# Applying the mean and the inverse deviation of two layer norms on the activation engine, one row tile later on the vector engine

## The reference, cut to what matters

```python
def _standardize(x):
    mu = mean(x); var = mean(square(x - mu))
    return (x - mu) * rsqrt(var + LN_EPS)

def _layer_norm(x, gain, bias):
    return _standardize(x) * gain + bias

# second block
x = _layer_norm(ALPHA * x + (1.0 + g1) * mix, ln1_gain, ln1_bias)
h = _standardize(x) * (1.0 + sc2) + sh2          # a second norm, of the result of the first
f = _conv_glu_ffn(h, w_ffn_up, w_ffn_conv, b_ffn_conv, w_ffn_down)
x = _layer_norm(ALPHA * x + (1.0 + g2) * f, ln2_gain, ln2_bias)   # this is the output
```

## Time and profile before

| what | value |
|---|---|
| median of 3 runs | 1673.8 us (1672.94 to 1674.36) |
| the profiled execution: time | 1674.36 us |
| its span, first to last instruction | 1672.4 us |
| PE busy | 1525.9 us, 91% of the span |
| DVE busy | 879.7 us, 53% |
| ACT busy | 582.6 us, 35% |
| POOL busy | 643.0 us, 38% |

### The profile page before, as it was taken

How to read it: one execution, slowest core, us unless ns; L and a number is a source line. 1 busy time by engine, 2 the same in 40 slices (tenths; PEclk the granted TensorE clock), 3 DMA queues, 4 the chain that set the end, 5 groups by cost and what they waited for, 6 DMA issues and landing times. The chain is left out here.

```text
span 1672.4 us, 19643 instructions
## 1 busy us (share of the span) xinstructions
PE 1525.9 (91%) x7216; PEld 1226.2 (73%) x7216; DVE 879.7 (53%) x1484; ACT 582.6 (35%) x856; POOL 643.0 (38%) x456
## 2 busy tenths in 40 slices
PE   4999989787999999997998999988994999999996
PEld 3776855676888788875877777777883888888885
DVE  4672378625858777397462255424548332333337
ACT  4332377115222121215341463444426332232231
POOL 2432200032655545562542224224551434544442
PEclk9999989898999999997997998998996999999998
DMA  7222000042655545222452633224421222223221
GB/s 273 88 92 78 26 26 2 1 164 97 212 189 198 205 151 189 101 76 82 113 149 78 173 103 131 89 87 171 138 76 76 76 101 101 84 93 105 97 101 51
DMA packets 48182, 185.72 MB, mean 111 GB/s; under 512 B 12960, under 2 KB 14112, under 8 KB 33248
## 3 DMA queue, kind: packets, MB, share of 16 engines
q1 hardware_dynamic: 30240, 165.53, 28.1%
q10 hardware_dynamic: 17856, 19.01, 4.1%
HBM read 169.71 MB, written 12.58 MB: 109 GB/s over the span
## 5 line engine op out<-in xcount | busy, mean ns | idle before, releaser
L1402 POOL TENSOR_TENSOR wlo<-raw,whi 128x512 fp32r<-128x512 f32 x448 | 637.3, 1453 | 997.0 <-ACT whi L898 997.0
L441 PE MATMUL bank<-Ahi,whi 128*128 128x512 f32 x1088 | 440.9, 405 | 22.0 <-issue 8.5
L442 PE MATMUL bank<-Alo,whi 128*128 128x512 f32 x1088 | 431.4, 397 | 0.0
L443 PE MATMUL bank<-Ahi,wlo 128*128 128x512 f32 x1088 | 431.2, 396 | 0.0
L898 ACT ACTIVATE whi<-raw 128x2048 fp32r<-128x2048 f32 x113 | 216.4, 1915 | 279.2 <-PE bank L471 216.9
L441 PEld LDWEIGHTS bank<-Ahi,whi 128*128 128x128 f32 x1088 | 210.1, 193 | 71.6 <-issue 17.4
L442 PEld LDWEIGHTS bank<-Alo,whi 128*128 128x128 f32 x1088 | 210.0, 193 | 45.1 <-issue 2.4
L443 PEld LDWEIGHTS bank<-Ahi,wlo 128*128 128x128 f32 x1088 | 208.9, 192 | 44.9
L469 PE MATMUL bank<-whi,Bhi 128*128 128x512 f32 x496 | 195.3, 394 | 5.6 <-POOL wlo L1402 5.6
L471 PE MATMUL bank<-whi,Blo 128*128 128x512 f32 x496 | 194.3, 392 | 0.0
L470 PE MATMUL bank<-wlo,Bhi 128*128 128x512 f32 x496 | 194.2, 392 | 0.0
(11 more groups left out here) (379 smaller groups left out, 1928.3 us busy)
## 6 DMA issues: line engine op xcount, KB each, us to landing
raw<-in_ws SPq DMA_DIRECT2D x113, 1024.0 KB, 5.0
adaw<-in_ada SPq DMA_DIRECT2D x48, 512.0 KB, 4.8
spill<-stage ACTq DMA_DIRECT2D x32, 256.0 KB, 2.0
X<-in_x SPq DMA_DIRECT2D x8, 512.0 KB, 6.2
gates<-spill SPq DMA_DIRECT2D x16, 256.0 KB, 2.9
w1k<-in_w1k SPq DMA_DIRECT2D x1, 2048.0 KB, 16.0
w1v<-in_w1v SPq DMA_DIRECT2D x1, 2048.0 KB, 20.2
XM<-spill ACTq DMA_DIRECT2D x8, 256.0 KB, 4.5
```

Of the source, the lines that this page charges most:

```text
L441: pe.matmul(ps[:], wh, hi[:, k], start=(k == 0), stop=False)
L442: pe.matmul(ps[:], wh, lo[:, k], start=False, stop=False)
L443: ins = pe.matmul(ps[:], wl, hi[:, k], start=False, stop=(k == kn - 1))
L1402: pool.tensor_tensor(wlo[slot][:, part], raw[slot][:, part], rd(whi[slot][:, part]), ALU.subtract).then_inc(sem("lo_split"), 1)
```

## The change

In both norms the subtraction of the mean and the product with the inverse deviation move from DVE to ACT, as one ACTIVATE in place on `X` (scale `sd`, bias `nmr`), which raises a new semaphore `ln_rows`. DVE forms `sd` and `nmr` first (`row_scale`, a reciprocal and a tiny product), and applies gain and bias in two passes without a per-row scalar (`tensor_tensor` mult, then `tensor_tensor` add, or in the mix stage `tensor_tensor_reduce`, which adds and sums). These two passes are done for the row tile before the current one, and a last pair follows after the loop.

```diff
@@ scalar engine @@
+            def plain_rows(i):
+                root(i, 2)
+                act.wait_ge(sem("rstd_ready"), A.due("rstd_ready"))
+                act.activation(X[:, i, :], X[:, i, :], ACT.Identity, scale=sd[:, i:i + 1],
+                               bias=nmr[:, i:i + 1]).then_inc(sem("ln_rows"), 1)
...
-            root(0, 2)
             for i in range(NT):
-                spread_of(i)
-                if i < NT - 1:
-                    root(i + 1, 2)
-                normed_row(i, 3)
-                if i == 0:
+                root(i, 2)
+                if i:
+                    spread_of(i - 1)
+                act.wait_ge(sem("rstd_ready"), A.due("rstd_ready"))
+                act.activation(X[:, i, :], X[:, i, :], ACT.Identity, scale=sd[:, i:i + 1],
+                               bias=nmr[:, i:i + 1]).then_inc(sem("ln_rows"), 1)
+                if i == 1:
                     hi_upto(last_tile(INDEX["mix.1.1"]) + 1)
+                if i:
+                    normed_row(i - 1, 3)
+            spread_of(NT - 1)
+            normed_row(NT - 1, 3)
...
             for i in range(NT):
-                root(i, 2)
+                plain_rows(i)
@@ vector engine @@
-            def centred(i):
-            def inverse_root(i):
...
             def gained(i):
+                dve.wait_ge(sem("ln_rows"), v.due("ln_rows"))
                 x = X[:, i, :]
-                stt(x, x, sd[:, i:i + 1], GB[:, 1], ALU.mult, ALU.add).then_inc(sem("x_final"), 1)
+                tt(x, x, GB[:, 0], ALU.mult).then_inc(sem("dve_step"), 1)
+                dve.wait_ge(sem("dve_step"), v.did("dve_step"))
+                tt(x, x, GB[:, 1], ALU.add).then_inc(sem("x_final"), 1)
                 dve.wait_ge(sem("x_final"), v.did("x_final"))
             def again(i):
+                dve.wait_ge(sem("ln_rows"), v.due("ln_rows"))
                 x = X[:, i, :]
-                dve.scalar_tensor_tensor(x, x, sd[:, i:i + 1], GB[:, 1], ALU.mult, ALU.add,
-                                         accum_out=tot[:, i:i + 1]).then_inc(sem("x_final"), 1)
+                tt(x, x, GB[:, 0], ALU.mult).then_inc(sem("dve_step"), 1)
+                dve.wait_ge(sem("dve_step"), v.did("dve_step"))
+                dve.tensor_tensor_reduce(x, x, GB[:, 1], 1.0, 0.0, ALU.add, ALU.add,
+                                         tot[:, i:i + 1]).then_inc(sem("x_final"), 1)
...
                 half_stats(i, 1)
                 row_stats(i, False)
                 if i:
+                    again(i - 1)
+                row_scale(i, False)
+                if i:
                     again_scale(i - 1)
-                centred(i)
-                inverse_root(i)
-                again(i)
+            again(NT - 1)
             dve.sem_inc(sem("gb_used"), 1)
             again_scale(NT - 1)
...
                         row_stats(i, False)
-                        centred(i)
-                        inverse_root(i)
-                        gained(i)
+                        row_scale(i, False)
+                        if i:
+                            gained(i - 1)
+            gained(NT - 1)
```

More of the change, by code:

```diff
@@ L2222, in _, with gained @@
                     spread("g1", G1b)
-            def centred(i):
+            def gained(i):
+                dve.wait_ge(sem("ln_rows"), v.due("ln_rows"))
                 x = X[:, i, :]
-                stt(x, x, mv[:, i, 0:1], GB[:, 0], ALU.subtract, ALU.mult).then_inc(sem("dve_step"), 1)
+                tt(x, x, GB[:, 0], ALU.mult).then_inc(sem("dve_step"), 1)
                 dve.wait_ge(sem("dve_step"), v.did("dve_step"))
-            def inverse_root(i):
[L2232 to L2238, removed]
-                stt(x, x, sd[:, i:i + 1], GB[:, 1], ALU.mult, ALU.add).then_inc(sem("x_final"), 1)
+                tt(x, x, GB[:, 1], ALU.add).then_inc(sem("x_final"), 1)
                 dve.wait_ge(sem("x_final"), v.did("x_final"))
             def again(i):
+                dve.wait_ge(sem("ln_rows"), v.due("ln_rows"))
                 x = X[:, i, :]
-                dve.scalar_tensor_tensor(x, x, sd[:, i:i + 1], GB[:, 1], ALU.mult, ALU.add,
-                                         accum_out=tot[:, i:i + 1]).then_inc(sem("x_final"), 1)
+                tt(x, x, GB[:, 0], ALU.mult).then_inc(sem("dve_step"), 1)
+                dve.wait_ge(sem("dve_step"), v.did("dve_step"))
+                dve.tensor_tensor_reduce(x, x, GB[:, 1], 1.0, 0.0, ALU.add, ALU.add,
+                                         tot[:, i:i + 1]).then_inc(sem("x_final"), 1)
                 dve.wait_ge(sem("x_final"), v.did("x_final"))
```

## The result

The changed kernel takes 1685.37 us (median of 14 executions, 1680.59 to 1687.59). The kernel before took 1676.58 (14 executions, the first three among them, 1672.94 to 1681.84), not the 1673.8 of those three. The ratio is 1.0051, 95% interval 1.004 to 1.0061: the change costs 8.5 us, and a later repetition of both on one chip gives 1.0049 (1.0034 to 1.0063), 8.2 us. Forecast were +8.7 us and 1682.5 us. The difference was met to within its uncertainty; the time itself lies 0.37 us above the stated range (1679.5 to 1685.0), because the level it was added to was too low.

A forecast was written before the change was run, and what follows sets the result against it. It took DVE's queue to bound both changed stages, where PE has run out of work. Mix +6.8 and end +1.9 us made +8.7 us on the median of 1673.8: 1682.5 us, range 1679.5 to 1685.

The forecast's parts named there:

- The wide passes: DVE in both stages: still two per row tile, each about 0.065 us shorter, 16 of them 1.0 us.
- The third rival: Both stages: passes without a row scalar take half the time, 0.64 us, total -0.9 us, 1672.9 us; chance 3%.
- The end stage: DVE's four end-stage row tiles: 22.9 us against 21.0, 5.73 each instead of 5.25, +1.9 us.
- The mix stage: DVE's last mean in the mix stage stands at 1286.0 instead of 1279.25: +6.8 us (5.3 to 8.3).
- The new wait: Mix stage, DVE before the again_scale reciprocal: 1.2 us idle for ACT's Square and root, three times.
- The wait for ACT's pass over the last row tile: Mix stage, after the loop: DVE idle 0.86 us before the last `again`.
- POOL's interference: Mix stage: POOL's pieces hold DVE's instructions, taken as 2.0 us (bounds 0.5 and 3.5).
- The undisturbed rest: Mix stage without POOL's interference, from the start at 1253.82 to the last mean at 1284.0 us.
- rival 1: POOL decides more, plus late outputs: mix +8.3 to +9, end +2.4, near 1685 us; chance 12%.
- rival 2: POOL's interference falls almost wholly into the new wait: mix +4.8, end +1.9, near 1680.5 us; chance 9%.
- rival 4: Mix stage's loss hidden because PE's restart hangs on something else: only +1.9 remains, 1675.7 us; chance 4%.
- the level of the sum: Whole kernel: the +8.7 us was added to the time before, taken as a median of 1673.8 us.

The follow-up runs named there:

- experiment 3: Changed kernel with DVE computing the second norm's scales one row tile later, behind the next add and statistics: mix stage 44.33 us instead of 46.38, ratio to before 1.0036.
- experiment 4: Changed kernel with the weight tile's high split moved behind ACT's loop over the row tiles: mix stage 45.75 us, ratio to before 1.0043.
- Experiment 9: The kernel before once more, unchanged: median 1677.05 us over 12 executions, ratio 0.9997.
- experiment 7: experiment 6 plus, for end-stage row tiles 0 to 2, mean and deviation on ACT, gain on DVE, bias on POOL: end stage 22.22 us, ratio to before 1.0000.
- experiment 5: Kernel before with only the end stage changed, the previous row tile's wide passes put in front of row_scale: end stage 23.04 us, ratio to before 1.0013.
- experiment 8: Changed kernel with second-norm scales later, weight split late and end-stage wide passes in front of row_scale: mix 43.20 us, end 23.04, ratio to before 1.0038.
- experiment 6: Kernel before with one weight tile's high split moved from behind row tile 0 to behind row tile 2: mix stage 38.45 us, ratio 0.9994.

## Why the prediction was right and wrong

**The wide passes** (16 times 0.065 us gained): right. 1.23 and 1.22 us after, 1.28 before. The third rival, passes at half the time, is refuted. The sentence of the Trainium skill that it came from ("Vector Engine (DVE) Microarchitecture Reference", "7. Points that are easy to get wrong") fails here: the float32 scalar_tensor_tensor is 5% dearer, not twice.

**The end stage**, +1.9 forecast, +1.88 measured, by the root that lost its cover (0.43 idle for each row tile, 0.40 more than the usual gap) and one tiny product of 0.20 more: four times 0.60, less eight passes that gain 0.065 each, is 1.88.

**The mix stage**, +6.8 forecast, +6.37 measured. The new wait was worked out as 1.2 and measured as 1.31 where POOL took no part, and experiment 3 gives two of the three back. The wait for ACT's pass over the last row tile was 0.78 (0.86 forecast). The term that was mis-sized is POOL's interference, 2.0 forecast and 1.37 measured in experiment 4, since the wait swallowed 0.55 us and only one wide pass was held. The undisturbed rest was 0.24 us too short (30.18 forecast from the start to the last mean, 30.42 in experiment 4), so part of the two errors cancels. By the stretches the whole change costs 8.25 us. That the whole times give 8.5, nearer to the 8.7, is luck: their interval reaches from 6.7 to 10.2 us.

**Rivals 1, 2 and 4.** POOL did not decide (rival 1), nor did its interference vanish (rival 2); the outputs issued closer together cost nothing that shows. The whole of the mix stage's loss arrives at PE's restart, so nothing hides it (rival 4).

**The step that failed is the last one, the level of the sum:** "by the median 1682.5 us". The three executions of before lay within 1.4 us, and I took their median as known and gave the range no term for it. Over 14 to 33 executions its median was 1676.6 to 1677.8, and from the fastest to the slowest it was 9 to 11 us. Experiment 9 shows where that comes from: its profiled execution took 3.4 us more than the one that the prediction used, with 2.85 us of it ahead of the mix stage and 0.60 in the stretch between, and the two stages of the change as long as there to 0.02 us. The first three are also the lowest three of the fourteen, which three drawn at random would be once in 364 draws; whether something set them apart, no run here shows. With 1676.6 the same sum gives 1685.3, against 1685.37 measured. The range of 5.5 us was made of the doubts about the difference alone, while the level was 3 to 4 us off.

## What to carry to other kernels

Before handing a step of a pipelined loop to an idle engine, ask whether a whole pass leaves the bound engine, and whether every result that comes back is asked for a good deal later than it is ordered. Here two passes stayed two, and a reciprocal that used to lie under other work was asked for 0.4 us after its 1.6 us of work had been ordered. No run here shows such a hand-over paying: in experiment 7 a whole pass did leave, and the engine that took over its work held the others. So before adding one, list what each engine has between order and use, for the last turn of the loop above all, where no next turn covers it (experiments 3, 5 and 8). And give the level of a predicted time a term of its own when it rests on three executions.

## What the runs showed of the hardware

POOL's tensor_tensor pieces hold DVE instructions with two SBUF inputs whatever their size: a product of one column took 0.27 to 1.16 us instead of 0.16 (the traces before and after, experiments 3, 4, 6, 7 and 8), an add of 512 columns up to 1.01 instead of 0.69 (1.47 for one just before the mix stage, in the trace of experiment 6), a pass of 1024 columns up to 2.39 instead of 1.28. The products that read PSUM (L1481) stayed at 0.69 beside POOL, and the reciprocals, with one input, at 0.16.

The hold ends with the piece that POOL is at. In the trace after, read in windows of 0.1 us, POOL's four pieces end near 1272.3, 1274.5 and 1275.8 and at 1276.97. The reduce pass begun at 1271.22 ends 1.1 us behind the first of them; the tiny products begun at 1273.83 and 1275.49 end at 1274.54 and 1275.76, with the second and the third; the add begun at 1276.52 ends 0.55 behind the fourth. And it goes both ways, for POOL's pieces get longer beside DVE's wide passes:

```profile
L1413 POOL TENSOR_TENSOR wlo<-raw,whi x4: 1255/1752/2259, 1270.1 to 1275.7; 128x512 fp32r<-128x512 f32 x4
```

The four took 6.91 us here and 5.39 before, against 4.93 in experiments 4, 6 and 8, where no wide pass ran beside them.

Moving the pieces away from the wide passes did not free the chain of them, since the tiny products between the engines are held too (by 0.73 us in experiment 4 and 0.63 in experiment 6).
